# A Strassen down projection: the third weight sum by an accumulating transfer, and eight quads in both column pairs

## What is computed

```python
def swiglu(h, w_gate, w_up, w_down):
    return (jax.nn.silu(h @ w_gate) * (h @ w_up)) @ w_down
...
    h = rms_norm(x, g_ffn[l])
    x = x + swiglu(h, w_gate[l], w_up[l], w_down[l])
return rms_norm(x, g_final)
```

## Time and profile before

| what | value |
|---|---|
| median of 3 runs | 1198.58 us (1197.51 to 1199.12) |
| the profiled execution, its own time | 1197.7 us |
| its span in the profile | 1196.0 us |
| mean granted TensorE clock | 0.998 |
| down projection, first PE step to the last | about 955 to 1182 us |
| matmul instructions | 5421 |
| bytes moved by DMA | 234.52 MB, mean 196 GB/s |

### The profile page before, as it was taken

The page is one execution under the profiler, slowest core; times in us unless marked ns, Lnnn a source line. Parts: engine busy times, 40 slices in busy tenths (PEclk is TensorE's granted clock), DMA queues, the critical chain, the costliest instruction groups (busy, mean ns, idle before and its releaser), DMA issues.

```text
span 1196.0 us, 16405 instructions
## 1 busy us (share of the span) xinstructions
PE 1184.9 (99%) x5421; PEld 982.6 (82%) x5421; DVE 930.3 (78%) x1171; ACT 673.6 (56%) x881; POOL 83.6 (7%) x89
## 2 busy tenths in 40 slices
PE   9999999999999999999999999999999999999997
PEld 7888888888888888888888888888888888888885
DVE  5755555557855666999899899989989889978886
ACT  5665555445744575756556555655555554545553
POOL 0042332200210000000000000000000000000000
PEclk9999999999999999999999999999999999999999
DMA  9865455556556544466666566566655666665663
GB/s 340 296 211 173 162 175 177 174 176 222 166 187 185 191 158 141 159 212 186 202 197 205 176 210 225 166 202 198 209 187 199 213 211 203 211 216 174 200 206 141
DMA packets 65851, 234.52 MB, mean 196 GB/s; under 512 B 7696, under 2 KB 8464, under 8 KB 65424
## 3 DMA queue, kind: packets, MB, share of 16 engines
q1 hardware_dynamic: 63072, 225.60, 57.6%
q10 hardware_dynamic: 2736, 8.35, 1.8%
HBM read 231.83 MB, written 2.10 MB: 196 GB/s over the span
## 4 chain that ended last, share of the span: by engine, by line
PE 93%; DVE 4%; DMA 1%; ACT 1%; issue 1%; SPq 0%; POOLq 0%; POOL 0%; ACTq 0%; DVEq 0%
PE ps L489 24%; PE ps L491 24%; PE ps L490 24%; PE ps L732 6%; PE ps L734 6%; PE ps L733 6%; DVE wlo L1624 2%; PE ps L521 1%; DMA raw<-w_stream 1%; DVE alo L1282 0%; PE ps L604 0%; DVE wlo L1270 0%; PE ps L559 0%; PE ps L564 0%; PE ps L688 0%
## 5 line engine op out<-in xcount | busy, mean ns | idle before, releaser
L1145 ACT ACTIVATE whi<-raw 128x1024 fp32r<-128x1024 f32 (+1 forms) x309 | 303.5, 992 | 216.6 <-PE ps L491 91.5
L1624 DVE TENSOR_TENSOR wlo<-raw,whi 128x1024 fp32r<-128x1024 f32 (+1 forms) x309 | 345.5, 1137 | 25.1 <-ACT whi L1145 24.3
L1270 DVE TENSOR_TENSOR wlo<-raw,whi 128x1024 fp32r<-128x1024 f32 x160 | 198.4, 1245 | 110.9 <-ACT whi L893 110.7
L489 PE MATMUL ps<-whi,ahi 128*128 128x512 f32 x600 | 235.6, 393 | 0.0
L491 PE MATMUL ps<-whi,alo 128*128 128x512 f32 x600 | 233.7, 390 | 0.0
L490 PE MATMUL ps<-wlo,ahi 128*128 128x512 f32 x600 | 233.5, 389 | 0.0
L893 ACT ACTIVATE whi<-raw 128x1024 fp32r<-128x1024 f32 x160 | 168.4, 1058 | 106.9 <-PE ps L491 94.0
L489 PE MATMUL ps<-whi,bhi 128*128 128x512 f32 x448 | 180.0, 402 | 1.5 <-DVE blo L1363 1.0
L491 PE MATMUL ps<-whi,blo 128*128 128x512 f32 x448 | 175.1, 391 | 0.0
L490 PE MATMUL ps<-wlo,bhi 128*128 128x512 f32 x448 | 174.5, 389 | 0.0
L491 PEld LDWEIGHTS ps<-whi,alo 128*128 128x128 f32 x600 | 112.6, 188 | 23.7
(11 more groups left out here) (244 smaller groups left out, 1488.1 us busy)
## 6 DMA issues: line engine op xcount, KB each, us to landing
raw<-w_stream SPq DMA_DIRECT2D x422, 512.0 KB, 4.1
res<-x_in ACTq DMA_DIRECT2D x4, 512.0 KB, 7.9
stage<-mem_in ACTq DMA_DIRECT2D x4, 512.0 KB, 6.1
proj<-mem_T ACTq DMA_DIRECT2D x2, 1024.0 KB, 7.8
stage<-x_T SPq DMA_DIRECT2D x7, 256.0 KB, 7.5
y_out<-res SPq DMA_DIRECT2D x4, 320.0 KB, 3.0
raw<-w_stream SPq DMA_DIRECT2D x4, 256.0 KB, 4.8
gfin<-g_final ACTq DMA_DIRECT2D x1, 1024.0 KB, 4.8
```

The costliest lines, as they stand in the source:

```text
L489: nc.tensor.matmul(bank, lhsT=a_h, rhs=w_h, start=start, stop=False)
L1145: nc.scalar.activation(whi_here, src, ACT.Copy).then_inc(hi_ready, 1)
L1270: vec.tensor_tensor(tile_pair(wlo, j), tile_pair(raw, j), tile_pair(whi, j).bitcast(f32), ALU.subtract).then_inc(lo_ready, 1)
L1624: vec.tensor_tensor(lo_here, src, hi_here.bitcast(f32), ALU.subtract).then_inc(lo_ready, 1)
```

## The change

1. Pair 0 gets eight quads (S0 to S7) in place of six, so steps 0 to 7 are quads in both pairs; plain steps 6 and 7 of pair 0 are gone.
2. The third weight sum is no longer made by DVE. ACT copies the sum b12 - b22 - b11 (its sign is turned, so that it can be added) twice beside each other into one of two buffers, `wsum` and `wsum2`, right behind its cast of part 2. Then POOL issues a transfer that reads the tile b11, b21 from the weight stream in HBM once more and adds it into that buffer (`accum_op=ALU.add`). 16 such transfers of 512 KB.
3. Part 3 is parted from its quad: `Z0` in the order is part 3 of quad 0. It stands behind the next quad's parts 0 to 2 (behind D18, or A18 and A19, for the last of a pair).
4. SP's load after part 1 waits for the split and no longer for the sum; the one after part 2 waits for the split and for ACT's copy.
5. `FORMS_AT` goes from positions 0, 14, 28, 50 to 0, 11, 22, 34: all four batches now fall in pair 0.
6. Signs of two forms are turned to fit.

```diff
-DOWN_ORDER = (("D6", "D7", "D8", "S0", "D9", "S1", "D10", "D11", "S2", "D12", "S3", "D13", "D14", "S4", "D15", "S5",
-               "D16", "D17", "D18", "D19", "D20", "D21"),
-              ("D8", "D9", "D10", "S0", "D11", "S1", "D12", "S2", "D13", "S3", "D14", "S4", "D15", "S5", "D16", "S6",
-               "D17", "S7", "A18", "A19", "A20", "A21", "B18", "B19", "B20", "B21"))
+DOWN_ORDER = ("D8 D9 D10 S0 D11 S1 Z0 D12 S2 Z1 D13 S3 Z2 D14 S4 Z3 D15 S5 Z4 D16 S6 Z5 D17 S7 Z6 D18 Z7 D19 D20 D21",
+              "D8 D9 D10 S0 D11 S1 Z0 D12 S2 Z1 D13 S3 Z2 D14 S4 Z3 D15 S5 Z4 D16 S6 Z5 D17 S7 Z6 A18 A19 Z7 A20 A21 "
+              "B18 B19 B20 B21")
...
-FORMS_AT = {0: 0, 14: 1, 28: 2, 50: 3}
+FORMS_AT = {0: 0, 11: 1, 22: 2, 34: 3}
...
             for i, (r, pair, q, n, part) in enumerate(DOWN):
-                if part == 1:
-                    sp.wait_ge(w_sums, DOWN_SUMS + 3 * n + 3)
-                elif part == 2:
+                if part == 2:
                     r += 1
                     sp.wait_ge(lo_ready, V_DN + i + 1)
-                elif part is None:
+                    sp.wait_ge(wsum_filled, n + 1)
+                elif part == 1 or part is None:
                     sp.wait_ge(lo_ready, V_DN + i + 1)
...
+            for n in range(QUAD_COUNT):
+                pool.wait_ge(wsum_filled, n + 1)
+                nc.gpsimd.dma_start(wsums[n % 2][:], stream[J_DN + DOWN[PART_AT[n, 1]][0]],
+                                    accum_op=ALU.add).then_inc(wsum_added[n % 2], 16)
...
+                elif part == 3:
+                    act.wait_ge(wsum_added[n % 2], 16 * (n // 2 + 1))
+                    src = wsums[n % 2][:]
...
+                    if part == 2:
+                        if n >= 2:
+                            act.wait_ge(lo_ready, V_DN + PART_AT[n - 2, QUAD_PARTS - 1] + 1)
+                        t2 = tile_pair(raw, J_DN + r + 1)[:, GC:KS * GC]
+                        nc.scalar.activation(wsums[n % 2][:].rearrange("p (h n) -> p h n", h=2),
+                                             t2.unsqueeze(1).to_broadcast([P, 2, GC]), ACT.Copy).then_inc(wsum_filled, 1)
...
-                if part == 1:
+                if part == 1 and n is None:
                     dve.wait_ge(w_sums, sums + 2)
                     both = b11_b21.rearrange("p (h n) -> p h n", h=2)
                     vec.tensor_tensor(wsum[:].rearrange("p (h n) -> p h n", h=2), both,
```

More of the change, by code:

```diff
@@ L81 @@
 for pair, order in enumerate(DOWN_ORDER):
-    for name in order:
+    for name in order.split():
         q = int(name[1:])
@@ L85 @@
             n = len([1 for place in DOWN if place[4] == 0])
-            DOWN += [(len(DOWN_TILES), pair, q, n, part) for part in range(QUAD_PARTS)]
+            DOWN += [(len(DOWN_TILES), pair, q, n, part) for part in range(QUAD_PARTS - 1)]
             DOWN_TILES += [(pair, q, 0), (pair, q, 1)]
+        if name[0] == "Z":
+            n = len([1 for place in DOWN if place[4] == QUAD_PARTS - 1])
+            DOWN.append((DOWN_TILES.index((pair, q, 0)), pair, q, n, QUAD_PARTS - 1))
         for half in {"D": (0, 1), "A": (0,), "B": (1,)}.get(name[0], ()):
@@ L92 @@
 PAIR_AT = [min(i for i, place in enumerate(DOWN) if place[1] == pair) for pair in range(2)]
-FIRST_QUAD = [min(i for i, place in enumerate(DOWN) if place[1] == pair and place[4] == 0) for pair in range(2)]
-LAST_QUAD = [max(i for i, place in enumerate(DOWN) if place[1] == pair and place[4] == 0) for pair in range(2)]
+PART_AT = {place[3:]: i for i, place in enumerate(DOWN) if place[4] is not None}
+QUAD_COUNT = len([1 for _, part in PART_AT if part == 0])
+FIRST_N = [min(place[3] for place in DOWN if place[1] == pair and place[4] == 0) for pair in range(2)]
+LAST_N = [max(place[3] for place in DOWN if place[1] == pair and place[4] == 0) for pair in range(2)]
+FIRST_QUAD = [PART_AT[n, 0] for n in FIRST_N]
+PRODUCTS_END = [PART_AT[n, QUAD_PARTS - 1] for n in LAST_N]
 GROUP_END = [max(i for i, place in enumerate(DOWN) if place[1] == g // 2 and place[4] is None and place[3] == g % 2)
@@ L827, in down_quad_part @@
                 v, (r, pair, q, n, part) = V_DN + i, DOWN[i]
-                opens, closes = i - part == FIRST_QUAD[pair], i - part == LAST_QUAD[pair]
+                opens, closes = n == FIRST_N[pair], n == LAST_N[pair]
                 left, right = quad_weights(v)
@@ L1127, in _, with part_cast @@
                                  asum[:, 1:QUAD_PARTS].rearrange("p f n m -> p (f n m)"), ACT.Copy).then_inc(s_hi, 1)
-            def part_cast(v, j, part, sums, vt=0, jt=0):
+            def part_cast(v, j, part, sums, vt=0, jt=0, n=None):
                 whi_here, src = whi[:, v % RING, :], tile_pair(raw, j)
@@ L1135, in part_cast @@
                     act.wait_ge(w_loaded[(j + 1) % RING], loaded_by(j + 1, jt))
-                if part in (2, 3):
+                if part == 2 or part == 3 and n is None:
                     act.wait_ge(w_sums, sums + part)
@@ L1139, in part_cast @@
                     src = tile_pair(raw, j + 1)
-                if part == 3:
+                if part == 3 and n is None:
                     src = wsum[:]
+                elif part == 3:
+                    act.wait_ge(wsum_added[n % 2], 16 * (n // 2 + 1))
+                    src = wsums[n % 2][:]
                 if part == 0:
@@ L1235, in _ @@
                 for pair in range(2):
-                    if i == LAST_QUAD[pair] + QUAD_PARTS - 1:
+                    if i == PRODUCTS_END[pair]:
                         down_p1_copy(pair)
@@ L1608, in combine, with part_split @@
                 vec.tensor_tensor(uu[:, 1, :], p5, uu[:, 1, :], ALU.add).then_inc(combined, 1)
-            def part_split(v, j, part, sums, vt=0):
+            def part_split(v, j, part, sums, vt=0, n=None):
                 hi_here, lo_here, src = whi[:, v % RING, :], wlo[:, v % RING, :], tile_pair(raw, j)
```

26 lines of the change are left out of this document (16 added, 10 removed).

## The result

| | before | after |
|---|---|---|
| median of 4 runs each | 1198.27 us (1197.51 to 1199.12) | 1231.85 us (1230.06 to 1232.9) |
| ratio, 95% interval | | 1.0278 (1.0261 to 1.0296) |
| the profiled execution's span | 1196.0 us | 1229.6 us |
| mean granted TensorE clock | 0.998 | 0.992 |

The account below looks back on a forecast made before the run. PE, busy 99% of the span, was taken to set the end: -1.36 - 0.78 + 5.5 = +3.4 on the profiled 1197.7 gave 1201.1, with the median 0.9 above, 1202.0 us; forecast 1200.6 to 1204.4, full range 1196.6 to 1209.

Parts of the forecast that it names:

- The quads: Two more quads in pair 0 each save PE 3 of 24 matmuls: -1.36 us, all on PE's path.
- the stalls of before: PE's stalls behind batches of forms in the kernel before, at places the change rewrites: -0.78 us.
- wsum off DVE: DVE saves 1.13 us a quad, so part 2's buffer reloads sooner; DVE's quad interval falls from 10.25 to about 9.2 us.
- The accumulating transfer beside the loads: POOL's transfer meets the load behind part 2; at 0.5 us added, the quads' interval is 9.7, under PE's 10.2: costs nothing.
- d: What the accumulating transfer adds to the landing of the load that decides: taken as 0.5 us, bounds 0 and 2.2.
- Its own landing: The accumulating transfer lands in 6 us (between 3.2 and 7.9); Z7 allows 8.7, other quads 12.1: hidden.
- lead: Time from DVE's first operation for a quad to PE's first matmul; before 3.79 to 5.39 us, 4.9 expected before batches.
- rival 3: The accumulating transfer itself lands late, Z7 stalling PE from 8.7 us on: 1208.6 at 12 us; chance 0.10.
- The forms: Batches of forms now stand in tight quads' periods in pair 0: +5.5 us on PE's path, 4.1 with d = 0.
- Ends of the pairs: `down_combine` comes about two tiles later, covered by six plain tiles in pair 0, ten in pair 1: nothing, else 5 us each.
- Rival 2: The load beside the transfer is slower than PE's pace, from d = 1.0; 1213.6 us at d = 2.2; chance 0.13.
- Rival 1: The leads hold and the batches hide, not slower: 1199.4 us, or 1196.5 with leads of 6.8 or more; chance 0.27.

Follow-up runs that it names:

- e7: Changed kernel with plain, overwriting transfers in place of the adding ones, issued by SP in its own queue right behind the load after part 2: 1205.11 us.
- e2: Changed kernel with the 16 POOL transfers written plainly, not added, so that the third sum is b11, b21 alone: 1216.82 us.
- e6: Changed kernel with plain, overwriting transfers issued from ACT's queue behind its copy, in place of POOL's adding ones: 1224.22 us.
- e1: Changed kernel without the 16 accumulating transfers, so the third sum lacks b11 and b21: 1203.39 us.
- e10: Changed kernel with the adding transfer cut to half the columns, 256 KB, so that b21 is left out of the sum: 1212.99 us.
- e4: Kernel before with eight quads in pair 0, the third sum still made by DVE and the batches of forms moved: 1200.08 us over 11 runs.

## Why the prediction was wrong in size

**The quads (-1.36) and the stalls of before (-0.78).** Right: 5415 matmuls, and the old places are gone; what stands in theirs is in the forms' sum.

**wsum off DVE.** Right in kind: in every run of the table whose quads wait for this load, the sum of the parts comes within 0.2 us of the interval. With 7.7 in the place of 4.3 the same sum that gave 9.2 gives 12.6.

**ACT's copy (0).** Right: the copy ends 3.94 us after the quad's start, DVE's split at 4.25, so the split releases SP's load.

**The accumulating transfer beside the loads: the step that failed.** The working said "Lower bound of d: 0 ... Upper bound: 2.2, were it as much work as two loads ... I take d = 0.5, half a load, since it overlaps only the later half." Measured, d is 3.4 (7.7 against 4.3), above the bound. Three things were wrong in it. *The overlap:* the transfer is issued 40 ns ahead of the load and lands 0.2 behind it, so it lies beside nearly the whole load. *The price of another transfer:* 1.1 was read from one queue, where the load in front pays next to nothing for those behind it. In e7 that nearly holds: 4.7 us against 4.3. In e2, from a second queue, the same bytes cost it 2.2, in e6 3.0. *The price of adding:* twice the engines' time per packet, as the bound supposed, which brings another 1.2; but the bound multiplied it with the price from one queue. 2.2 + 1.2 gives the 3.4.

The Trainium skill's rule that was weighed there ("DMA: Bandwidth & Descriptors", Queues, rings and completion order), that a DMA engine takes turns between the queues packet by packet, pointed the right way: a transfer on another queue does slow the load, and by more than the 1.1 that the working took from it. The turns themselves are not shown. The rows of e2's section have equal counts over 4 us, 102 and 100 packets side by side; but of these, 1145.5 to 1147 has 59 of POOL's and 32 of SP's, and e6 has a us with 75 of ACT's and none of SP's, and the trace doesn't say which engine a packet ran on. What is shown is the outcome: where the two were issued together from two queues, they ended together. The row of one queue was the wrong one to choose d by.

**Its own landing (6, hidden).** 7.9 measured, the long end of the range given. Under the limit of 12.1, so hidden for most; for Z7 the 8.7 supposed a lead of 4.9, and with 1.44 it is less: there are two waits for the added sum, up to 5.8 us on ACT, and PE loses 1.9 and 1.5 us there. Part of rival 3.

**The forms (+5.5 at d = 0.5, 4.1 at d = 0).** Right with no transfer: 5.2 measured in e1, at the three places named. In the kernel after they cost 15.5, because leads there are 1.4 to 1.8 and a batch has nothing to hide behind. The working had the rule for this (a lead of 3.2, then 4.4) but a landing that was too good.

**Ends of the pairs (nothing).** 1.36 us in e1, 1.3 to 2.0 in e2, e7 and e10. The working counted ten plain tiles behind `down_combine` in pair 1; the order has six behind Z7 (A20, A21, B18 to B21), of which DVE has split three before the combination and gets only two more done before the next result is due. That is too few to catch up the combination's 4.9 us.

**Rival 2** was the right mechanism: it named the wrong sign as "loads that land over 5.3 us behind part 2, with leads that shrink through pair 1". It was capped by the same bound, so it reached 1213.6 only. Its 2.4, the lead below which PE stalls at part 1, fits: with leads of 1.44 PE starts part 1 0.9 us late, as at 1152.75 above. With d = 3.4 its own formula gives 2.4 us for each single quad; that is the 12.6 against 10.2 of the trace. **Rival 1** is dead: no quad of pair 1 but the first has a lead over 3.94. Rival 2's doubt about POOL slowing DVE is settled too: a split of 1024 columns takes 1.22 us as before.

**The slow matmuls.** The working had no term for them. Behind stalls of 0.9 to 2.4 us, 27 matmuls ran at the lower clock, about 6 us, part of which PE would have waited anyway.

Of the 33.6 us: e1 accounts for 5.2 (batches 5.2 and the end 1.4, less the two quads' 1.36), a transfer on a second queue for 13.4 (e2 less e1), its adding for 15.0 (after less e2).

**Open:** why a plain transfer from a second queue costs the load 2.2 us, and from ACT's 3.0, when its packets take only 1.5 us of all engines. A part of it is time in which the engines aren't full: in e2's pair above they are busy for 48% of the us from 1145.5, and for 96% from 1146.5 to 1150. Open too is how an adding transfer does its work inside an engine; only its time per packet was seen.

## What to carry to other kernels

A load that the critical chain waits for should share its moments with nothing on another queue: the bytes of the newcomer are paid by the load, whatever the mean DMA share says (0.64 in e1's pair 1, 206 GB/s, where e7 had room for 257). If more bytes must come, put them behind the load in its own queue (11.7 us better here), and if that can't be, let them start when it has nearly landed, and then look at which load they meet next. Work taken off an engine that has time to spare (DVE, 78% busy) was worth little here: with the sum on DVE and eight quads in pair 0 (e4) the kernel takes 1200.08 us, and with the sum gone and the change's order (e1) 1203.39. Price first what the substitute does to the wait that ends last.

## What the runs showed of the chip that was not expected

- An accumulating DMA holds the DMA engines twice as long as a plain one with the same packets: 19.2% against 9.4% of 16 engines over 250 us, for 8.39 MB.
- Two transfers of 512 KB issued together from two queues end together, 0.2 us apart: 6.3 and 6.5 us (plain), 7.8 and 8.1 (one adding). In one queue the first lands after 4.7 and the second after 5.6.
- Plain transfers from ACT's queue slowed a load of SP's more than those from POOL's, 7.3 against 6.3 (medians 7.3 and 6.5). ACT's, issued 0.3 us ahead of the load, had the engines alone for a whole us.
- Adding transfers of half the bytes in the same number of packets held the engines as long as plain ones of all of them, 9.6% against 9.4%.
